# Half of the output projection's products of four token tiles computed inside Hyena's transform stage

## The chip, the cores and the metric

The kernel runs on one core of one Trainium2 chip. The metric is the device time of one execution in microseconds. Engines are called as in the profile: PE (TensorE, matmuls), DVE (VectorE), ACT (ScalarE), POOL (GpSimd) and SP (SyncE, which here issues the DMAs).

## The reference

One layer of a diffusion backbone over 1024 latent tokens of width 1024 and 256 context tokens. Four token mixers read one normalised input; their outputs, 256 columns each, are joined and go through one output projection. A routed mixture of 16 experts follows.

```python
ya_c, ya_l = gla_mixer(...)
yb_c, yb_l = hyena_mixer(...)
yc_c, yc_l = mamba_mixer(...)
yd_c, yd_l = deltanet_mixer(...)
y_l = jnp.concatenate([ya_l, yb_l, yc_l, yd_l], axis=-1) @ w_out[i]
x = x + (g1 * rmsnorm(y_l, norm_g[i, 1]).astype(F32)).astype(x.dtype)
h_l = modulate(x, norm_g[i, 2], sh2, sc2)
m_l = ec_moe(h_l, moe_router[i], moe_w_gate[i], moe_w_up[i], moe_w_down[i])
x = x + (g2 * rmsnorm(m_l, norm_g[i, 3]).astype(F32)).astype(x.dtype)
```

Hyena convolves its input twice with long filters, each time by a transform of length 2 x 1024, a product with the filter's spectrum and an inverse transform:

```python
def long_conv(u, h_fwd, h_bwd, d_skip):
    spec = jnp.fft.rfft(u, n=2 * l_, axis=1) * jnp.fft.rfft(kern, axis=0)[None]
    y = jnp.fft.irfft(spec, n=2 * l_, axis=1)[:, :l_]
    return y + u * d_skip
z = x1 * long_conv(v, h[:, 0, 0], h[:, 0, 1], d[0])
return (x2 * long_conv(z, h[:, 1, 0], h[:, 1, 1], d[1])).astype(u.dtype)
```

## The kernel before

The program is a row of stages. Every stage gives each engine its own list of instructions, which it runs in the order written; semaphores tie the lists together, and a stage begins when all engines have ended the one before. Nothing reorders work at run time, so the order around the change is what the code of a stage says.

Four stages matter. `hy_f` makes the filters' spectra by matmuls and, at its end, the transforms of Hyena's first two units. `hy_d` (called the transform stage below) does the rest of Hyena. `out` is the output projection with the router. Then `moe` runs the experts, one after the other.

**The transform stage.** Work is cut into eight units u = 4 o + 2 g + b: the convolution o, the half g of the 256 columns, the half b of the frequencies. For each unit PE makes the forward transform (`forward`, L2791, here called spectrum(u)), ACT copies one half of it out of PSUM (`hy_odd`, L3039), and DVE does sixteen operations, L3053 to L3079: two that add and subtract the halves (`hy_ab`, `hy_cd`, one operand in PSUM), and fourteen with both operands in SBUF, the product with the spectrum of the filter among them. Between groups of these DVE waits for its own last result, six times in a unit. Then PE makes the inverse transform inverse(u) (L3005, or L3010 in the second convolution), which adds into PSUM banks 4 and 5 for g = 0 and 6 and 7 for g = 1. When both b of a half are in, DVE multiplies them by the gate: `gated(g)` (L3083, into `hy_v`) after the first convolution, `result(g)` (L3091, into `yT`) after the second. DVE's order is unit 0, 1, 2, gated(0), 3, 4, gated(1), 5, 6, result(0), 7, result(1). PE's order is spectrum 2 and 3, inverse 0, 1 and 2, spectrum 4 and 5, inverse 3 and 4, spectrum 6 and 7, inverse 5, 6 and 7. POOL has nothing to do in this stage. SP loads the inverse's table and `w_out` in two halves of 2 MB, the first rows (k below 4) after spectrum(7), because their place is in use until then.

**The projection.** y = yT' w_out with 8 token tiles t of 128 and 8 blocks k of 128 input columns. Float32 is reached by three products of rounded halves: with hi the operand copied to the matmul's rounded type (ACT) and lo the rest (a subtraction on DVE or POOL), each block adds hi x hi, hi x lo and lo x hi, for two halves of 512 output columns. So a tile has 8 x 3 x 2 = 48 matmuls of 128x512 (L3221 to L3223). `w_out` is split at the start, eight blocks, by ACT (L3279) and DVE (L3316). `yT` is split tile by tile: `yT_hi` by ACT (L3284), `yT_lo` by POOL (L3176).

Behind the products of tile t comes a chain: squares and root of y on ACT (L3263, L3265), scaling on DVE (L3369, `res_tmp`), the residual sum on POOL (L3182, `x`), squares and root again on ACT (L3270, L3272), scaling on DVE (L3354, `h`), a row added on POOL (L3185, `h`) and a store for the experts. PE transposes x (`turn_rows`, L3196), ACT and DVE copy the transposes (`h2T`, L3300, L3341), and PE multiplies them by the router (L3209); softmax and a transpose of the affinities follow (L3293, L3336, L3217).

The lists fix who goes first. On PE, tile t is: half of its products, the router of tile t-2, the other half, turn_rows(t-1), the affinities' transpose of t-3. Before its first product PE waits for `yT_lo` of tile t. On POOL the order is yT_lo(t+1), x(t), h(t), yT_lo(t+2), x(t+1), and so on. On ACT it is yT_hi(t+1), the exponential of t-2, h2T(t-1), squares of y(t), squares of x(t). Two tiles use PSUM banks 0 to 3 in turn.

Of the kernel before, what the change touches and what calls it, by code (L numbers as in the profile page):

```python
# [15 lines left out]
F32 = mybir.dt.float32  # L16
# [2734 lines left out]
def hyena(nc, S, A, norm):  # L2751
# [43 lines left out]
    fwd_in, y_back = nc.alloc_semaphore("hy_fwd_in"), nc.alloc_semaphore("hy_y_back")  # L2795
    with Stage(nc, "hy_f", "tables turn_in d_in centre conv_1 conv_2 x2 taps tapped first skipped mixed even odd copied turned added_even "
# [13 lines left out]
        def _(sp):  # L2810
# [144 lines left out]
    S.w_out = Plan(nc, S.hT_at + KD * D * 4, S.stage_at).take("w_out", [P, KD, D])  # L2955
    plan = Plan(nc, high)
    with Stage(nc, "hy_d", "tab w_out fwd even odd_half ab x p yc pq w inv z fin") as s:
# [7 lines left out]
        X8 = X[:, :, :, :].rearrange("p s q c -> p (s q) c")  # L2965
        UNITS = [(u, u // (2 * BT), u // BT % 2, u % BT) for u in range(4 * BT)]

        def load_out(sp, h):
            sp.dma_start(S.w_out[:, 4 * h:4 * h + 4, :],
                         A["w_out"][0, 512 * h:512 * h + 512, :].rearrange("(k p) n -> p k n", p=P)).then_inc(s.w_out, 16)  # L2970

        @s.block.sync
        def _(sp):
            for q in range(2):
                sp.dma_start(inv[:, q, :, :], A["dft_inv"][q].rearrange("(t p) k -> p t k", p=P)).then_inc(s.tab, 16)
            load_out(sp, 1)
# [7 lines left out]
        def _(pe):  # L2984
# [30 lines left out]

            spectrum(2)
# [15 lines left out]
        @s.block.scalar
        def _(act):
            for u, o, g, b in UNITS:
# [72 lines left out]
    SPENT.extend([fwd_in, win_in, y_back] + S.hy_w)  # L3107
# [3 lines left out]
KEPT = (0, 1, 4, 5)  # L3111


def project_out(nc, S, A):
# [3 lines left out]
    xt = [low.take(f"res_x{b}", [P, D]) for b in range(2)]  # L3118
    tm = [low.take(f"res_tmp{b}", [P, D]) for b in range(2)]
    yh = [low.take("yT_hi0", [P, KD, P], F32R)]  # L3120
    yl = nc.alloc_sbuf_tensor_at("yT_lo", [P, KD, SEQ], F32R, offset=S.yT_at)
    wl = nc.alloc_sbuf_tensor_at("w_out_lo", [P, KD, D], F32R, offset=S.hT_at + KD * D * 4)
# [4 lines left out]
    wh = low.take("w_out_hi", [P, KD, D], F32R)  # L3127
# [9 lines left out]
    with Stage(nc, "out", "rows_in r_in x_in*2 y ss rt y_sc x1d ss2 rt2 h2m h2d h2s*2 tr ht_a ht_v lg mx ex af at at_o "  # L3137
                          "chain zero zst yh yl wh wl rr_in rr_t rc rs shift shifted x1h lgd h2l") as s:
# [751 lines left out]
```

## Time and profile before

| | us |
|---|---|
| median of 3 runs | 1743.55 |
| lowest and highest | 1738.53 and 1744.39 |
| the profiled execution | 1743.24 |
| its span, first to last instruction | 1741.4 |
| granted PE clock, mean over the span | 0.946 of full speed |
| busy: PE, DVE, ACT, POOL | 1540.7, 1207.1, 919.7, 307.9 |
| PE's share of the span | 88% |

The profile gives times from the start of the span. The transform stage lies from 871.5 to 957 us, the projection from 957 to 1087, the experts behind it. A line such as `1046.46 0.50 PE L3221 MATMUL ... [0.20 <-POOL yT_lo L3176]` reads: at 1046.46 us, for 0.50 us, PE ran line 3221 of the kernel, after 0.20 us of idling that POOL's write of yT_lo (line 3176) ended. Matmuls overlap, so their durations (0.39) are longer than the distance from one start to the next (0.227). In a merged row "x32" stands for 32 instructions, and the duration covers all of them.

### The profile page before, as it was taken

The numbers are of one execution on the slowest core, as the hardware profiler recorded it, in microseconds if no ns is written. First come the engines' busy times: TensorE is split into PE (matmuls) and PEld (weight loads), VectorE is DVE, ScalarE is ACT, GpSimd is POOL, SyncE is SP. The second block draws the span as 40 slices with busy tenths as digits, with TensorE's granted clock in tenths as the row PEclk, the third lists the DMA queues.
The fourth block names the chain that finished last, engine by engine and source line by source line (L and its number), as shares of the span: only waits on it lengthen the run. The fifth ranks groups of instructions, "written<-read, shape, count | busy, mean of one in ns | idle before, by whom it ended". The sixth has DMA issues, their size and how long they took to land. (4 is left out here: it accounts for less than half of the span.)

```text
span 1741.4 us, 21707 instructions
## 1 busy us (share of the span) xinstructions
PE 1540.7 (88%) x8298; PEld 1258.9 (72%) x8298; DVE 1207.1 (69%) x1403; ACT 919.7 (53%) x1308; POOL 307.9 (18%) x371
## 2 busy tenths in 40 slices
PE   6899999988989699998976999199999999999991
PEld 3686788777877589876475787078888888888871
DVE  4872754395655556665798534888888888888873
ACT  5441364375446376543100444167777777777753
POOL 0300500160016685000000443000100010001001
PEclk9999999998998899999988998599999999999996
DMA  9571210050018544211121522389999999999967
GB/s 351 165 263 55 114 49 1 25 168 27 1 41 256 185 113 122 89 32 61 61 97 49 208 96 74 153 341 394 392 376 402 395 389 381 401 396 395 377 216 217
DMA packets 109098, 345.13 MB, mean 198 GB/s; under 512 B 37501, under 2 KB 46998, under 8 KB 84419
## 3 DMA queue, kind: packets, MB, share of 16 engines
q1 hardware_dynamic: 99534, 320.34, 48.6%
q0 software_dynamic: 5328, 18.88, 4.5%
q10 hardware_dynamic: 4133, 4.53, 1.0%
q8 instruction: 66, 1.08, 0.3%
q14 instruction: 37, 0.30, 0.1%
HBM read 301.14 MB, written 37.32 MB: 194 GB/s over the span
## 5 line engine op out<-in xcount | busy, mean ns | idle before, releaser
L3635 DVE TENSOR_TENSOR w_lo<-w_raw,w_hi 128x2048 fp32r<-128x2048 f32 x192 | 438.1, 2291 | 64.1 <-ACT w_hi L3577 64.1
L3577 ACT ACTIVATE w_hi<-w_raw 128x2048 fp32r<-128x2048 f32 x192 | 368.1, 1918 | 142.9 <-PE ps L3522 132.7
L3520 PE MATMUL ps<-w_hi,xsT_hi 128*128 128x512 f32 x512 | 202.1, 395 | 1.1 <-DVE xsT_lo L3640 1.1
L3522 PE MATMUL ps<-w_hi,xsT_lo 128*128 128x512 f32 x512 | 199.8, 390 | 0.0
L3521 PE MATMUL ps<-w_lo,xsT_hi 128*128 128x512 f32 x512 | 199.5, 390 | 0.0
L3488 POOL DMA_INDIRECT moe_sum<-y,idx_col x15 | 30.3, 2021 | 461.0 <-ACT y L3597 430.0
L3520 PEld LDWEIGHTS ps<-w_hi,xsT_hi 128*128 128x128 f32 x512 | 96.2, 188 | 20.6 <-DVE xsT_lo L3640 1.5
L3522 PEld LDWEIGHTS ps<-w_hi,xsT_lo 128*128 128x128 f32 x512 | 96.1, 188 | 20.3
L3521 PEld LDWEIGHTS ps<-w_lo,xsT_hi 128*128 128x128 f32 x512 | 96.2, 188 | 19.3
L3520 PE MATMUL ps<-w_hi,hiddenT_hi 128*128 128x512 f32 x256 | 99.7, 390 | 0.6 <-DVE hiddenT_lo L3652 0.6
L3521 PE MATMUL ps<-w_lo,hiddenT_hi 128*128 128x512 f32 x256 | 99.6, 389 | 0.0
L3522 PE MATMUL ps<-w_hi,hiddenT_lo 128*128 128x512 f32 x256 | 99.6, 389 | 0.0
L3176 POOL TENSOR_TENSOR yT_lo<-yT,yT_hi 128x1024 fp32r<-128x1024 f32 x7 | 18.4, 2629 | 231.4 <-ACT yT_hi L3284 231.4
L3520 PEld LDWEIGHTS ps<-w_hi,hiddenT_hi 128*128 128x128 f32 x256 | 48.0, 188 | 11.0 <-DVE hiddenT_lo L3652 1.0
L3522 PEld LDWEIGHTS ps<-w_hi,hiddenT_lo 128*128 128x128 f32 x256 | 48.0, 188 | 10.0
L3521 PEld LDWEIGHTS ps<-w_lo,hiddenT_hi 128*128 128x128 f32 x256 | 48.0, 188 | 10.0
L3221 PE MATMUL ps<-w_out_hi,yT_hi 128*128 128x512 f32 x128 | 52.2, 408 | 2.1 <-POOL yT_lo L3176 2.1
L655 PE MATMUL ps<-hT_lo,mb_w_hi 128*128 128x512 f32 x128 | 50.5, 395 | 0.0
L3222 PE MATMUL ps<-w_out_lo,yT_hi 128*128 128x512 f32 x128 | 50.4, 394 | 0.0
L3223 PE MATMUL ps<-w_out_hi,yT_lo 128*128 128x512 f32 x128 | 50.3, 393 | 0.0
L1876 POOL TENSOR_TENSOR dn_block_inv<-dn_block_inv,dn_block_tmp 128x247 f32<-128x247 f32 (+15 forms) x82 | 46.8, 571 | 6.4
L757 ACT ACTIVATE mb_c_line<-ps 128x512 f32<-128x512 f32 (+1 forms) x20 | 18.3, 917 | 52.7 <-PE ps L660 49.9
(610 smaller groups left out, 3612.2 us busy)
## 6 DMA issues: line engine op xcount, KB each, us to landing
w_raw<-in_moe_w_gate SPq DMA_DIRECT2D x64, 1024.0 KB, 6.5
w_raw<-in_moe_w_up SPq DMA_DIRECT2D x64, 1024.0 KB, 8.2
w_raw<-in_moe_w_down SPq DMA_DIRECT2D x64, 1024.0 KB, 8.5
w_mod_row<-in_w_mod SPq DMA_DIRECT2D x32, 512.0 KB, 4.9
w_mod<-in_w_mod SPq DMA_DIRECT2D x8, 1024.0 KB, 17.6
dn_ma<-dn_ma SPq DMA_DIRECT2D x16, 512.0 KB, 4.0
dn_mT<-dn_ma SPq DMA_DIRECT2D x20, 256.0 KB, 3.6
x_tile<-in_x SPq DMA_DIRECT2D x8, 512.0 KB, 16.0
```

The lines of the kernel that those rows point to most:

```text
L655: nc.tensor.matmul(pairs(c), ring[:, i % 2, k, :], S.h_low[:, k, t0:t0 + 512].rearrange("p (a b) -> p a b", a=2), start=False, stop=False)
L1876: last = ops.tensor_tensor(bd[:, j + 1:DB, 0:c], bd[:, j + 1:DB, 0:c], t, ALU.subtract)
L3176: nc.gpsimd.tensor_tensor(tile_cols(yl, t + 1), tile_cols(S.yT, t + 1), yh[(t + 1) % 2][:, :, :], ALU.subtract).then_inc(s.yl, 1)
L3221: nc.tensor.matmul(out, yh[t % 2][:, k, :], wh[:, k, c], start=(k == 0), stop=False)
L3222: nc.tensor.matmul(out, yh[t % 2][:, k, :], wl[:, k, c], start=False, stop=False)
L3223: return nc.tensor.matmul(out, yl[:, k, t * P:(t + 1) * P], wh[:, k, c], start=False, stop=(k == KD - 1))
L3488: pool.indirect_dma_start(A["moe_sum"], bass.IndirectOffsetOnAxis(ap=S.icol[:, u:u + 1], axis=0), y[:, :], None, compute_op=ALU.add).then_ ...
L3520: nc.tensor.matmul(out, h[:, kk, :], wh[w][:, c:c + 512], start=kk == 0, stop=False)
L3521: nc.tensor.matmul(out, h[:, kk, :], wl[w][:, c:c + 512], start=False, stop=False)
L3522: last = nc.tensor.matmul(out, l[:, kk, :], wh[w][:, c:c + 512], start=False, stop=kk == KD - 1)
L3577: nc.scalar.activation(wh[q % RING][:, :], S.raw[q % RAW][:, :], ACT.Copy).then_inc(s.hi, 1)
L3635: nc.vector.tensor_tensor(wl[q % RING][:, :], S.raw[q % RAW][:, :], wh[q % RING][:, :].bitcast(F32), ALU.subtract).then_inc(s.lo, 1)
```

## The change

For the four odd token tiles (`PART`), the products of blocks 4 to 7, whose `yT` columns come from mixers that are done before (`y_kept`), are computed in the transform stage, and added in the projection.

- SP: the half of `w_out` with blocks 4 to 7 is loaded at the end of `hy_f`, when its last odd products are done.
- ACT in the transform stage: after `even` of unit 0 four copies that make `w_out_hi_rest`; after that of unit 1 four that make the odd tiles' `yT_hi_part` (128x512 each); later four copies `put(j)` of results (128x1024) out of PSUM banks 6 and 7 into `y_part`.
- POOL in the transform stage: four subtractions of 128x1024 (`w_out_lo`) and four of 128x512 (`yT_lo`), each waiting for ACT's copy.
- PE in the transform stage: `part(j)`, 24 matmuls of 128x512 each into banks 6 and 7: part(0) after inverse(1), part(1) after inverse(3), part(2) after inverse(5), part(3) after inverse(6).
- Banks 6 and 7 are now the parts', so both halves g use banks 4 and 5, and inverse(2), inverse(4) and inverse(6) first wait for gated(0), gated(1) and result(0).
- The projection: odd tiles have 24 matmuls and half-sized splits; DVE adds `y_part` to their PSUM banks before ACT squares them; `w_out` has four blocks to split; even tiles begin with blocks 4 to 7.

The diff, cut to its core:

```diff
@@ hyena, stage hy_f @@
+            sp.wait_ge(s.odd, BT)
+            load_out(sp, 1)
@@ stage hy_d, sync @@
-            load_out(sp, 1)
-
             sp.wait_ge(s.fwd, 4 * BT - 2)
             load_out(sp, 0)
@@ tensor @@
             def inverse(u):
                 u, o, g, b = UNITS[u]
                 pe.wait_ge(s.w, u + 1)
+                if b == 0 and (o, g) == (0, 1):
+                    pe.wait_ge(s.z, 1)
+                if b == 0 and (o, g) == (1, 0):
+                    pe.wait_ge(s.z, 2)
+                if b == 0 and (o, g) == (1, 1):
+                    pe.wait_ge(s.fin, 2)
                 for r in range(CLASSES):
-                    bank, at = 4 + 2 * g + r // 2, (r % 2) * 256
+                    bank, at = 4 + r // 2, (r % 2) * 256
...
+            def part(j):
+                pe.wait_ge(s.w_lo, 4)
+                pe.wait_ge(s.y_lo, j + 1)
+                if j:
+                    pe.wait_ge(s.put, j)
+                y_low = tile_of(yl, PART[j])
+                for k in range(4):
+                    for h in range(2):
+                        out, c = S.ps[:, 6 + h, :], slice(h * 512, h * 512 + 512)
+                        nc.tensor.matmul(out, yh[j][:, k, :], wh[:, k, c], start=(k == 0), stop=False)
+                        nc.tensor.matmul(out, yh[j][:, k, :], wl[:, 4 + k, c], start=False, stop=False)
+                        last = nc.tensor.matmul(out, y_low[:, k, :], wh[:, k, c], start=False, stop=(k == 3))
+                last.then_inc(s.part, 1)
@@ scalar @@
+                if u == 0:
+                    act.wait_ge(w_out_in, 16)
+                    for k in range(4):
+                        nc.scalar.activation(wh[:, k, :], wo[:, 4 + k, :], ACT.Copy).then_inc(s.w_hi, 1)
+                if u == 1:
+                    act.wait_ge(y_back, 16 * len(KEPT))
+                    for j, t in enumerate(PART):
+                        nc.scalar.activation(yh[j][:, :, :], tile_of(S.yT, t), ACT.Copy).then_inc(s.y_hi, 1)
+                if u in (3, 5):
+                    put(u // 2 - 1)
+            put(2)
+            put(3)
@@ gpsimd @@
+            for k in range(4):
+                pool.wait_ge(s.w_hi, k + 1)
+                nc.gpsimd.tensor_tensor(wl[:, 4 + k, :], wo[:, 4 + k, :], wh[:, k, :], ALU.subtract).then_inc(s.w_lo, 1)
+            for j, t in enumerate(PART):
+                pool.wait_ge(s.y_hi, j + 1)
+                nc.gpsimd.tensor_tensor(tile_of(yl, t), tile_of(S.yT, t), yh[j][:, :, :], ALU.subtract).then_inc(s.y_lo, 1)
@@ project_out @@
+        cut = lambda t: slice(0, 4 if t in PART else KD)
+        def order(t):
+            return (0, 1, 2, 3) if t in PART else (4, 5, 6, 7, 0, 1, 2, 3)
@@ vector @@
+                if t in PART:
+                    dve.wait_ge(s.y, t + 1)
+                    y = S.ps[:, 2 * (t % 2):2 * (t % 2) + 2, :].rearrange("p a b -> p (a b)")
+                    nc.vector.tensor_tensor(y, y, S.part[PART.index(t)][:, :], ALU.add).then_inc(s.joined, 1)
                 if t >= 1:
                     turn(t - 1)
```

How the instructions stand, at three places. PE in the transform stage, from the forward transforms at the end of `hy_f` on; the products with `yT_hi_part` are the first of part(0), eight such threes in all:

```order
 L2791 MATMUL ps<-hy_v,hy_fwd 128x128 x64
-L3005 MATMUL ps<-hy_w,hy_inv 128x128 x48
+L3024 MATMUL ps<-hy_w,hy_inv 128x128 x32
+L3044 MATMUL ps<-w_out_hi_rest,yT_hi_part_9303 128x512
+L3045 MATMUL ps<-w_out_lo,yT_hi_part_9303 128x512
+L3046 MATMUL ps<-w_out_hi_rest,yT_lo 128x512
```

Three inverses stood in a row; now a part stands between the second and the third, and in the same way behind inverse(3), inverse(5) and inverse(6).

POOL, from the last stage before Hyena's spectra into the projection, before:

```order
 L559 MEMSET hy_c_line_8443 128x1
-L3176 TENSOR_TENSOR yT_lo<-yT,yT_hi_9775 128x8x128
-L3182 TENSOR_TENSOR x_89<-res_tmp_9765,res_x_9763 128x1024
-L3185 TENSOR_TENSOR h_0_9770<-h_0_9770,row_broadcasts 128x1024
-L3176 TENSOR_TENSOR yT_lo<-yT,yT_hi_9767 128x8x128
```

and now:

```order
+L3099 TENSOR_TENSOR w_out_lo<-w_out,w_out_hi_rest 128x1024 x4
+L3102 TENSOR_TENSOR yT_lo<-yT,yT_hi_part_9303 128x4x128
+L3102 TENSOR_TENSOR yT_lo<-yT,yT_hi_part_9304 128x4x128
+L3102 TENSOR_TENSOR yT_lo<-yT,yT_hi_part_9305 128x4x128
+L3102 TENSOR_TENSOR yT_lo<-yT,yT_hi_part_9306 128x4x128
+L3242 TENSOR_TENSOR yT_lo<-yT,yT_hi_9929 128x4x128
+L3248 TENSOR_TENSOR x_89<-res_tmp_9927,res_x_9925 128x1024
+L3251 TENSOR_TENSOR h_0_9920<-h_0_9920,row_broadcasts 128x1024
+L3242 TENSOR_TENSOR yT_lo<-yT,yT_hi_9919 128x8x128
```

Eight subtractions of the transform stage stand ahead of the projection's; in the projection the subtraction for an odd tile is half as large (4 blocks), that for an even tile is the same.

## Rows read from the trace of the kernel before

**Rows 1.** Windows, the two stages: PE, PEld, DVE, ACT, POOL busy; clock, DMA.

```profile
871.50:957.00 85.50, 60.52 (x384) 56.15 (x384) 78.53 (x135) 4.78 (x8) 0.00 (x0) 0.86 0.20 74
957.00:1087.00 130.00, 122.39 (x617) 101.82 (x617) 58.79 (x100) 63.37 (x103) 51.60 (x21) 0.95 0.35 126
```

**Rows 2.** Timeline of DVE, transform stage: start, us, line, [idle before <-releaser].

```profile
872.28 0.69 DVE L3053 TENSOR_TENSOR hy_ab<-ps,hy_odd 128x512 f32<-128x512 f32 x1 [0.78 <-ACT hy_odd L3039]
...
881.47 0.68 DVE L3053 TENSOR_TENSOR hy_ab<-ps,hy_odd 128x512 f32<-128x512 f32 x1
...
899.81 1.21 DVE L3083 TENSOR_TENSOR hy_v<-hy_x,ps 128x1024 f32<-128x1024 f32 x1
...
938.77 2.07 DVE L3091 TENSOR_TENSOR yT<-yT,ps 128x512 f32<-128x512 f32 x2
...
953.88 1.10 DVE L3091 TENSOR_TENSOR yT<-yT,ps 128x512 f32<-128x512 f32 x1 [3.87 <-PE ps L3010]
```

**Rows 3.** Timeline of PE, transform stage.

```profile
873.72 6.43 PE L2791 MATMUL ps<-hy_v,hy_fwd 128*128 128x128 f32 x32 [5.36 <-DVE hy_cd L3054]
...
899.95 5.33 PE L3005 MATMUL ps<-hy_w,hy_inv 128*128 128x128 f32 x32 [4.64 <-DVE hy_w L3079]
...
912.26 3.74 PE L3005 MATMUL ps<-hy_w,hy_inv 128*128 128x128 f32 x32
...
938.91 3.72 PE L3010 MATMUL ps<-hy_inv,hy_w 128*128 128x256 f32 x16 [3.47 <-DVE hy_w L3079]
950.06 5.80 PE L3010 MATMUL ps<-hy_inv,hy_w 128*128 128x256 f32 x16 [7.43 <-DVE hy_w L3079]
```

**Rows 4.** Timeline of PE in the projection, around the starts of tiles.

```profile
1002.06 1.03 PE L3196 MATMUL ps<-tables,x 128*128 128x128 f32 x8
...
1017.80 0.50 PE L3221 MATMUL ps<-w_out_hi,yT_hi 128*128 128x512 f32 x1 [0.74 <-POOL yT_lo L3176]
...
1028.66 0.39 PE L3221 MATMUL ps<-w_out_hi,yT_hi 128*128 128x512 f32 x1
...
1030.70 1.03 PE L3196 MATMUL ps<-tables,x 128*128 128x128 f32 x8
...
1046.46 0.50 PE L3221 MATMUL ps<-w_out_hi,yT_hi 128*128 128x512 f32 x1 [0.20 <-POOL yT_lo L3176]
```

**Rows 5.** Timeline of ACT and POOL, the chain behind tile 2.

```profile
1005.61 0.29 ACT L3265 ACTIVATE out_stats<-out_stats,eps 128x1 f32<-128x1 f32 x1
...
1007.49 2.37 POOL L3182 TENSOR_TENSOR x<-res_tmp,res_x 128x1024 f32<-128x1024 f32 x1 [6.08 <-DVE res_tmp L3369]
...
1013.04 2.39 POOL L3185 TENSOR_TENSOR h<-h,row_broadcasts 128x1024 f32<-128x1024 f32 x1 [3.17 <-DVE h L3354]
...
1015.38 2.36 POOL L3176 TENSOR_TENSOR yT_lo<-yT,yT_hi 128x1024 fp32r<-128x1024 f32 x1
```

**Rows 6.** Timelines of ACT and DVE around the squares of tile 7.

```profile
1073.74 1.02 ACT L3263 ACTIVATE squares<-ps 128x1024 f32<-128x1024 f32 x1 [1.05 <-PE ps L3223]
...
1071.40 1.37 DVE L3336 TENSOR_SCALAR aff<-aff,out_stats 128x16 f32<-128x16 f32 x1
```

**Rows 7.** Windows, ahead of inverse(7); columns as in rows 1.

```profile
948.00:950.00 2.00, 0.00 (x0) 0.00 (x0) 1.97 (x5) 0.00 (x0) 0.00 (x0) 0.50 0.00 0
```

**Rows 8.** Where POOL's and DVE's operations meet: timelines, one row of a source view.

```profile
959.55 9.16 DVE L3316 TENSOR_TENSOR w_out_lo<-w_out,w_out_hi 128x1024 fp32r<-128x1024 f32 x8
...
966.79 4.17 POOL L3176 TENSOR_TENSOR yT_lo<-yT,yT_hi 128x1024 fp32r<-128x1024 f32 x1 [231.38 <-ACT yT_hi L3284]
...
L3322 DVE TENSOR_TENSOR router_scaled<-router,row_cols x2: 277/1278/2278, 968.8 to 971.0; 128x128 f32<-128x128 f32 x2
...
75.14 3.95 POOL L989 TENSOR_TENSOR hT_lo<-hT,hT_hi_end 128x512 fp32r<-128x512 f32 x2
...
75.85 8.49 DVE L1213 SCALAR_TENSOR_TENSOR mod_acc<-w_mod_row,silu_cond,mod_acc 128x1024 f32<-128x1024 f32 x5
```

**Rows 9.** DMA view, 800 to 975 us: KB each, median us from issue to landing.

```profile
w_out<-in_w_out SPq DMA_DIRECT2D x2, 2048.0 KB, 9.8
```

More of the change, by code:

```diff
@@ L2954, in hyena @@
     assert low.at <= S.hT_at + KD * D * 4
-    S.w_out = Plan(nc, S.hT_at + KD * D * 4, S.stage_at).take("w_out", [P, KD, D])
+    S.w_out_low = nc.alloc_sbuf_tensor_at("w_out_lo", [P, KD, D], F32R, offset=S.hT_at + KD * D * 4)
+    S.y_low = nc.alloc_sbuf_tensor_at("yT_lo", [P, KD, SEQ], F32R, offset=S.yT_at)
+    S.w_out_rest = nc.alloc_sbuf_tensor_at("w_out_hi_rest", [P, 4, D], F32R, offset=low.at)
+    assert low.at + 4 * D * 4 == S.hT_at + KD * D * 4
+    wo, wl, wh, yl = S.w_out, S.w_out_low, S.w_out_rest, S.y_low
+    yh = [nc.alloc_sbuf_tensor_at(f"yT_hi_part{j}", [P, 4, P], F32R, offset=S.stage_at - (4 - j) * 2048)
+          for j in range(len(PART))]
+    S.part = [nc.alloc_sbuf_tensor_at(f"y_part{j}", [P, D], F32, offset=at)
+              for j, at in enumerate((SBUF_END - 8288, SBUF_END - 4192, S.spare_at, S.spare_at + 4096))]
     plan = Plan(nc, high)
-    with Stage(nc, "hy_d", "tab w_out fwd even odd_half ab x p yc pq w inv z fin") as s:
+    with Stage(nc, "hy_d", "tab fwd even odd_half ab x p yc pq w inv z fin w_hi w_lo y_hi y_lo part put") as s:
         W = plan.take("hy_w", [P, 2, BT, CLASSES, 2, P])
@@ L3020, in _ @@
             inverse(1)
+            part(0)
             inverse(2)
@@ L3024, in _ @@
             inverse(3)
+            part(1)
             inverse(4)
@@ L3028, in _ @@
             inverse(5)
+            part(2)
             inverse(6)
+            part(3)
             inverse(7)
@@ L3033, in _, with put @@
         def _(act):
+            def put(j):
+                act.wait_ge(s.part, j + 1)
+                nc.scalar.activation(S.part[j][:, :], S.ps[:, 6:8, :].rearrange("p a b -> p (a b)"), ACT.Copy).then_inc(s.put, 1)
             for u, o, g, b in UNITS:
@@ L3117, in project_out @@
     rows = low.take("row_broadcasts", [P, 3, D])
-    xt = [low.take(f"res_x{b}", [P, D]) for b in range(2)]
-    tm = [low.take(f"res_tmp{b}", [P, D]) for b in range(2)]
     yh = [low.take("yT_hi0", [P, KD, P], F32R)]
-    yl = nc.alloc_sbuf_tensor_at("yT_lo", [P, KD, SEQ], F32R, offset=S.yT_at)
-    wl = nc.alloc_sbuf_tensor_at("w_out_lo", [P, KD, D], F32R, offset=S.hT_at + KD * D * 4)
+    yl, wl = S.y_low, S.w_out_low
     low = Plan(nc, S.hT_at + 2 * KD * D * 4)
@@ L3126, in project_out @@
     st = low.take("out_stats", [P, LT, 8])
-    wh = low.take("w_out_hi", [P, KD, D], F32R)
+    w_first = low.take("w_out_hi_first", [P, 4, D], F32R)
+    wh = [w_first[:, k, :] for k in range(4)] + [S.w_out_rest[:, k, :] for k in range(4)]
+    xt = [low.take(f"res_x{b}", [P, D]) for b in range(2)]
+    tm = [low.take(f"res_tmp{b}", [P, D]) for b in range(2)]
     yh.append(low.take("yT_hi1", [P, KD, P], F32R))
@@ L3230, in _ @@
             pe.wait_ge(s.yl, 1)
-            for k in range(KD):
-                pe.wait_ge(s.wl, k + 1)
+            for k in order(0):
+                if k < 4:
+                    pe.wait_ge(s.wl, k + 1)
                 for h in range(2):
@@ L3248, in _ @@
                     if t < LT:
-                        for k in range(KD):
+                        for k in order(t):
                             last = product(t, h, k)
@@ L3277, in _ @@
             nc.scalar.activation(yh[0][:, :, :], tile_cols(S.yT, 0), ACT.Copy).then_inc(s.yh, 1)
-            for k in range(KD):
-                nc.scalar.activation(wh[:, k, :], wo[:, k, :], ACT.Copy).then_inc(s.wh, 1)
+            for k in range(4):
+                nc.scalar.activation(wh[k], wo[:, k, :], ACT.Copy).then_inc(s.wh, 1)
             for t in range(LT + 2):
@@ L3313, in _ @@
             nc.vector.tensor_tensor(tile_cols(yl, 0), tile_cols(S.yT, 0), yh[0][:, :, :], ALU.subtract).then_inc(s.yl, 1)
[L3314 removed]
+            for k in range(4):
                 dve.wait_ge(s.wh, k + 1)
[L3316 removed]
+                nc.vector.tensor_tensor(wl[:, k, :], wo[:, k, :], wh[k], ALU.subtract).then_inc(s.wl, 1)
             dve.wait_ge(s.rr_t, 1)
```

43 lines of the change are left out of this document (27 added, 16 removed).

## The prediction

> **What bounds the kernel now.** I read the stretches first: the Hyena transform stage (871.5 to 957 us) and the output projection (957 to 1087 us) [rows 1]. In the transform stage DVE is busy for 78.5 of 85.5 us and PE for 60.5. The rows of DVE there show why: a unit (16 operations) takes 9.19 us (872.28 to 881.47), one follows the other without a gap, and DVE has its only long wait (3.87 us) at the end, for PE's inverse(7) [rows 2]. So DVE sets this stage, PE has gaps of 3.4 to 7.4 us [rows 3], and work that goes into the gaps is free only if it keeps DVE free as well.
>
> In the output projection PE is busy for 122.4 of 130 us [rows 1], which looks like the bound. The rows around the tiles' starts say something finer [rows 4]. y(t) is the moment at which a tile's products end, read off the transposes that follow. Tile 2 ends at 1002.06 and tile 4 starts at 1017.80, released by POOL's yT_lo; tile 4 ends at 1030.70 and tile 6 starts at 1046.46, released by the same; 15.74 and 15.76 us. Between lies a chain over four engines [rows 5]: turn_rows (1.0) and ACT's h2T, squares and root to 1005.90, DVE's res_tmp, POOL's x to 1009.86, ACT's squares and root again, DVE's h, POOL's h to 1015.43, and only then POOL's yT_lo of tile t+2 to 1017.74. An even tile's own products and router take 12.9 us (1017.80 to 1030.70). So start(t+2) = start(t) + 12.9 + 15.7 = 28.6 us for two tiles; the rows give 1046.46 - 1017.80 = 28.66. PE is full there because the odd tile between happens to fill the 15.7 us: the loop through POOL is already the bound, and PE is level with it.
>
> **The change part by part.**
>
> *Products out of the projection.* Four tiles lose 24 of 48 products. At 0.227 us from one to the next (1028.66 to 1030.70 for nine) that is 5.45 us a tile, 21.8 us of PE's time. The tiles are the odd ones. An even tile still has 48 products, and its chain still ends with a whole yT_lo, so even tiles still start 28.6 us apart. The odd tile's 5.45 us becomes a longer wait of PE. I book 0 of the 21.8 us for tiles 1, 3 and 5.
>
> *Tile 7.* Here nothing of an even tile follows, so 5.45 us could show. But ACT comes to the squares of y(7) at 1073.74 only 0.2 us after PE, behind squares of x(6), an exponential and two table loads; DVE reaches its new addition only after the affinity of tile 5, which ends at 1072.77 [rows 6]. The addition of 128x1024 costs about 1.2 us (DVE's hy_v, with one PSUM operand, takes 1.21 [rows 2]), so it ends near 1074.0 and the squares begin 0.3 us later than before. Gain 0, loss 0.3 to 0.5; up to 2 if the router's and the transposes' small products there run at the lower clock. I take 0.5.
>
> *PE's new wait inside the projection.* After tile t (even) PE now does turn_rows, half a tile with a router and another turn_rows: 1.3 + 5.45 + 1.7 + 1.0 = 9.4 us, and then waits for the rest of the 15.7 us: 6.3 us, before tiles 4 and 6, and about as long before tile 2, whose products wait for the same subtraction behind tile 0's chain. What such a wait costs can be read in the transform stage: after 7.43 us of idling inverse(7) took 5.80 us where inverse(6), the same sixteen, took 3.72 [rows 3], and the granted clock had fallen to 0.50 by 948 to 950 [rows 7]. That is the level of 1.2 GHz in place of 2.4. Against 3.74 for 32 products at full clock, the wait of 5.36 us cost 2.7 and that of 4.64 cost 1.6; the wait of 3.47 cost nothing [rows 3]. I take 2.1 for each of three restarts, 6.3 us, on the path, since the even tile's products are a link of the loop. Bounds 0 and 3 x 2.7 = 8.1.
>
> *ACT in the transform stage.* Four copies of 128x1024 after `even` of unit 0, four half as large after that of unit 1, and four copies of results; ACT's pass over 128x1024 takes 1.02 us [rows 6], so some 10 us in all. ACT is otherwise busy for 4.8 of 85.5 us [rows 1]; the copy for unit 1 is needed at 881.47 and now comes near 872.2 + 4 x 1.02 = 876.3. Free. The load of w_out that they wait for is now issued in the stage before, when its last odd products have ended; such a load takes 9.8 us [rows 9]. Were it 3 us late, the copy for unit 1 would still be in time. Free.
>
> *POOL in the transform stage.* Eight subtractions with two SBUF operands, four of 128x1024 (2.37 us each when alone) and four of half that. They run beside DVE, which is the bound, and 14 of the 16 operations of a unit read two SBUF operands. The trace shows what this does [rows 8]. POOL's subtraction issued at 966.79 took 4.17 us, waited until DVE's w_out_lo series had ended (968.71) and then ran to 970.96; DVE's router_scaled, issued at 968.82, took 2.278 us where its twin took 0.277: 2.0 us lost. At 75.14 two POOL subtractions of 128x512 went in between five chained DVE operations: 8.49 us for five of some 1.2 each (as hy_v's 1.21), so 2.4 lost, about 1.2 for each. Both engines stand still for one another, a whole instruction at a time, and POOL gets its turn where DVE waits for its own last result. A unit has six such places, so POOL's eight go through in units 0 and 1. The first starts behind ACT's first copy, near 873.3, and costs 2.0; three more at about 2.25 (968.71 to 970.96) cost 6.75; of the small ones one falls on a pair that reads PSUM (hy_ab, hy_cd) and three cost 1.2. Sum 12.3; the small ones' share is the least sure, and I use 12. Bounds: 0, if DVE were not held, and 4 x 2.37 + 4 x 1.2 = 14.3. Nothing hides it: from unit 2 on everything shifts.
>
> The Trainium skill, "SBUF — State Buffer", section "Who interferes with whom", says that the second port pair is an exclusive lock, that a VectorE operation with two SBUF inputs and a GpSimd operation contend for it, and that the loser waits for the whole instruction. By that rule alone the eight would cost their whole length, 14.3 in place of 12 (1763 in place of 1761); the rows agree with it in kind, and the difference is the part that runs beside operations with a PSUM operand.
>
> *Two banks for both halves.* inverse(2), inverse(4) and inverse(6) now wait for DVE's reading of the banks. Before, inverse(2) began at 899.95 and inverse(6) at 938.91, and DVE's readings ended at 901.02 and 940.84 [rows 2, 3]. They move by 1.1 and 1.9 us (with the parts ahead of them not much more), and PE then has to finish spectrum(4) and spectrum(6) before units 4 and 6. Counted through with products of 0.227 us and full clock: spectrum(6) ends 0.9 us before unit 6 wants it. Cost 0. Behind inverse(6), part(3) ends some 0.6 us after unit 7: +0.6.
>
> *A warm end.* part(3) runs right up to inverse(7), which then takes 3.7 instead of 5.8 us and is on the path [rows 2, 3]: -2.1.
>
> **Sum.** Transform stage +12.0 + 0.6 - 2.1 = +10.5; projection +6.3 + 0.5 = +6.8; together +17.3 us. The profiled execution took 1743.24 us with a span of 1741.4, the median is 1743.55. Behind the projection come DVE's selection and the experts, which only start later. 1743.55 + 17.3 = 1760.9; I say 1761, 1.0% slower.
>
> **The rivals.**
> 1. *No holding of DVE* (POOL's subtractions slip in without cost): transform stage -1.5, projection +6.8, 1749. For it: w_out_lo's eight ran on at 1.15 us each (9.16 in all) with POOL already waiting [rows 8]. Against: those were a series without waits, a unit is not. 0.10.
> 2. *No fall of the clock in the projection's waits*: 1743.55 + 10.5 + 0.5 = 1754.5. For it: the one wait of 3.47 us that cost nothing; against: all three waits of over 4 us cost 1.6 or more. 0.12.
> 3. *POOL starves*: it gets its turn only beside hy_ab and hy_cd, once per unit. Then yT_lo's first part is ready only after unit 3, part(0) holds back inverse(2) and spectrum(4) in PE's queue, and unit 4, due at 910, would start after 1.2 (the subtraction) + 7.5 (part(0), half of it at the lower clock) + 3.7 + 3.7 us of work from 914 on, near 930: +20 and 3.6 of holding beside the pairs, less the 2.1 at the end, with 6.8 in the projection: near 1771. 0.08.
> 4. *PE is the bound of the projection, so it is faster*: the 21.8 us come off, with 10.5 us of the transform stage against them: 1732. It decides from the point where the chain to yT_lo takes less than an odd tile's stay on PE (9.4 us after the change, and it takes 15.7). For it: 122 of 130 us busy, and waits for yT_lo of only 0.74 and 0.20 us [rows 1, 4]. Against: the two equal intervals of 28.6 us. 0.06.
>
> **How the numbers follow.** Forecast 0.64, rivals 0.10, 0.12, 0.08 and 0.06. The range runs from rival 1 to the forecast with the upper bounds (14.3 for 12, 8.1 for 6.3, 2 for 0.5: 1767): 1748 to 1767, with the forecast, rival 2 and most of rival 1, 0.83. A measurement of this kernel can tell about 0.3% (5.2 us) from no change. Faster by more: 0.05; within: 0.08 (rival 1 ends on this edge); slower: 0.87.
>
> **What would show it.** In the profile after: DVE's units 0 and 1 together 30 us instead of 18, with single operations of 2.5 us or more beside POOL's; units 2 to 7 at 9.2 us as before; PE's last inverse at 3.7 us; even tiles starting 30 to 31 us apart and waiting about 6 us for yT_lo, with a granted clock near 0.5 behind each wait; DVE's new addition before ACT's squares of tile 7. I am wrong if even tiles start much less than 28 us apart, or if units 0 and 1 keep their 9.2 us.

## The result and the profile after

The changed kernel took 1762.98 us in the median of 4 runs (1760.93 to 1764.0), the kernel before 1743.9 us in 4. The ratio is 1.0109, with a 95% interval of 1.0094 to 1.0125: slower by 19.1 us. The prediction was 1761 us, slower, in a range of 1748 to 1767.

The profiled execution of the changed kernel took 1762.85 us with a span of 1761.0, 19.6 more than before. I cut both spans at the same three marks: the start of ACT's first `hy_odd` (start of the transform stage), its first `yT_hi` of the projection, and DVE's first MAX8 of the selection that follows. For the kernel before these windows are (columns as in [rows 1]: start and end, length, busy PE, PEld, DVE, ACT, POOL, granted clock, DMA):

```profile
871.58:957.05 85.47, 60.52 (x384) 56.15 (x384) 78.53 (x134) 4.78 (x8) 0.00 (x0) 0.86 0.20 74
957.05:1088.55 131.50, 122.39 (x617) 101.82 (x617) 58.79 (x101) 63.37 (x103) 51.60 (x21) 0.94 0.35 125
```

and for the changed kernel:

```profile
872.35:968.18 95.83, 76.90 (x480) 70.00 (x480) 90.97 (x134) 14.62 (x20) 17.32 (x8) 0.88 0.12 44
968.18:1107.80 139.62, 109.20 (x521) 90.37 (x521) 54.77 (x101) 57.96 (x99) 45.37 (x21) 0.85 0.33 118
```

| part | before | after | difference |
|---|---|---|---|
| up to the transform stage | 871.58 | 872.35 | +0.8 |
| transform stage | 85.47 | 95.83 | +10.4 |
| projection | 131.50 | 139.62 | +8.1 |
| from the selection to the end of the span | 652.9 | 653.2 | +0.3 |

The 0.8 us ahead of the transform stage tell nothing. In the ten profiles of this case that stage begins between 870.9 and 875.9 us; the four kernels that load `w_out` where the kernel before does span that whole range, the six that load half of it earlier lie inside it.

So the projection has lost 13 us of PE's busy time (122.39 to 109.20, with 96 products fewer) and has become 8.1 us longer. In the transform stage DVE does the same 134 operations in 90.97 us instead of 78.53, and POOL, idle before, is busy for 17.32.

**Transform stage.** DVE's unit 0 in the changed kernel; the first row is one of the pair with an operand in PSUM, the other (L3116) is left out. In the kernel before such a unit took 9.19 us [rows 2]:

```profile
873.04 0.69 DVE L3115 TENSOR_TENSOR hy_ab<-ps,hy_odd 128x512 f32<-128x512 f32 x1 [0.78 <-ACT hy_odd L3080]
...
874.37 2.32 DVE L3120 TENSOR_TENSOR hy_x<-hy_ab 128x256 f32<-128x256 f32 x1
876.61 2.59 DVE L3121 TENSOR_TENSOR hy_x<-hy_ab 128x256 f32<-128x256 f32 x1
879.12 2.56 DVE L3122 TENSOR_TENSOR hy_x<-hy_cd 128x256 f32<-128x256 f32 x1
881.61 2.56 DVE L3123 TENSOR_TENSOR hy_x<-hy_cd 128x256 f32<-128x256 f32 x1
884.20 2.17 DVE L3126 TENSOR_TENSOR hy_p<-hy_x,hy_k_cos 128x1024 f32<-128x1024 f32 x1
886.29 2.28 DVE L3126 TENSOR_TENSOR hy_p<-hy_x,hy_k_sin 128x1024 f32<-128x1024 f32 x1
888.60 1.63 DVE L3131 TENSOR_TENSOR hy_p<-hy_p,hy_p 128x512 f32<-128x512 f32 x1
890.16 1.74 DVE L3132 TENSOR_TENSOR hy_p<-hy_p,hy_p 128x512 f32<-128x512 f32 x1
...
894.61 0.68 DVE L3115 TENSOR_TENSOR hy_ab<-ps,hy_odd 128x512 f32<-128x512 f32 x1
```

and all of POOL's work in that stage:

```profile
874.04 9.85 POOL L3099 TENSOR_TENSOR w_out_lo<-w_out,w_out_hi_rest 128x1024 fp32r<-128x1024 f32 x4 [138.27 <-ACT w_out_hi_rest L3085]
883.85 7.51 POOL L3102 TENSOR_TENSOR yT_lo<-yT,yT_hi_part 128x512 fp32r<-128x512 f32 x4
```

Eight of DVE's operations, one after the other, are long, and POOL has eight subtractions. The unit takes 894.61 - 873.04 = 21.57 us, 12.38 more than 9.19. From 894.61 on units take 9.2 us again. At the end of the stage PE's last inverse, inverse(7), runs at full clock:

```profile
963.26 3.72 PE L3029 MATMUL ps<-hy_inv,hy_w 128*128 128x256 f32 x16
```

It took 5.80 us before [rows 3] and now takes 3.72. That gives back 2 us: 12.38 - 2.0 = 10.4.

**Projection.** The starts and ends of tiles on PE; an end is read off the transposes (`tables,x`) that follow, as in [rows 4]:

```profile
1000.19 0.79 PE L3291 MATMUL ps<-w_out_hi_rest,yT_hi 128*128 128x512 f32 x1 [6.57 <-POOL yT_lo L3242]
1000.78 0.63 PE L3292 MATMUL ps<-w_out_lo,yT_hi 128*128 128x512 f32 x1
1001.21 0.63 PE L3293 MATMUL ps<-w_out_hi_rest,yT_lo 128*128 128x512 f32 x1
...
1005.88 0.40 PE L3292 MATMUL ps<-w_out_lo,yT_hi 128*128 128x512 f32 x1
1006.12 0.40 PE L3293 MATMUL ps<-w_out_hi_first,yT_lo 128*128 128x512 f32 x1
...
1015.68 1.03 PE L3262 MATMUL ps<-tables,x 128*128 128x128 f32 x8
...
1031.39 0.79 PE L3291 MATMUL ps<-w_out_hi_rest,yT_hi 128*128 128x512 f32 x1 [6.15 <-POOL yT_lo L3242]
...
1046.66 1.03 PE L3262 MATMUL ps<-tables,x 128*128 128x128 f32 x8
...
1062.36 0.79 PE L3291 MATMUL ps<-w_out_hi_rest,yT_hi 128*128 128x512 f32 x1 [4.12 <-POOL yT_lo L3242]
...
1077.50 1.03 PE L3262 MATMUL ps<-tables,x 128*128 128x128 f32 x8
```

Even tiles start 31.20 and 30.97 us apart, where [rows 4] have 28.66. From the end of tile 2 to the start of tile 4 it is 15.71 us and from tile 4 to tile 6 15.70, as before (15.74, 15.76): the chain over ACT, DVE and POOL has kept its length. What has grown is the tile itself, 12.90 before, now 15.49, 15.27 and 15.14. Behind the first product, twelve start 0.43 us apart (as 1000.78 and 1001.21), the later ones about 0.23 (1005.88 to 1006.12). The granted clock in the windows says the same (columns as above):

```profile
996.00:998.00 2.00, 0.00 (x0) 0.00 (x0) 1.08 (x2) 1.41 (x3) 2.00 (x2) 1.00 0.00 0
1002.00:1004.00 2.00, 2.00 (x6) 1.54 (x5) 0.00 (x0) 1.47 (x4) 0.46 (x1) 0.50 0.52 199
```

PE is idle from 993.6 on. At 996 to 998 the clock still stood at 2.4 GHz (1.00); behind the wait it stands at 1.2 GHz (0.50). PE's waits for `yT_lo` in one view (in total, how often, the longest):

```profile
PE ps L3291 <- POOL yT_lo L3242: 16.8, 3, 6.6
```

They came to 2.1 us in three waits before. Another wait is new: behind tile 7 PE has no work until the router, and finds itself at the lower clock there:

```profile
1094.11 3.57 PE L3275 MATMUL ps<-router_scaled,h2T 128*128 128x16 f32 x16 [5.04 <-ACT h2T L3375]
```

Before, the row at this place was:

```profile
1075.81 2.32 PE L3209 MATMUL ps<-router_scaled,h2T 128*128 128x16 f32 x16 [0.90 <-ACT h2T L3300]
```

### The profile page after: what moved, and what is told of

The parts are those of the page before. It is cut to its first block and busy times, and to the rows that moved or that the text cites. A ratio compares the mean times of both kernels' runs of the same rounds, so it can differ in the third digit from the quotient of the medians.

```text
span 1761.0 us, 21736 instructions
## 1 busy us (share of the span) xinstructions
PE 1545.7 (88%) x8298; PEld 1262.9 (72%) x8298; DVE 1217.1 (69%) x1403; ACT 924.6 (53%) x1316; POOL 319.5 (18%) x379
## 5 line engine op out<-in xcount | busy, mean ns | idle before, releaser
L2791 PE MATMUL ps<-hy_v,hy_fwd 128*128 128x128 f32 x256 | 33.9, 300 | 20.6 <-DVE hy_cd L3116 20.6
L2791 PEld LDWEIGHTS ps<-hy_v,hy_fwd 128*128 128x128 f32 x256 | 33.5, 215 | 21.5 <-DVE hy_cd L3116 15.4
L1874 POOL TENSOR_TENSOR dn_block_tmp<-dn_block_l,dn_block_inv 128x247 f32<-128x247 f32 (+15 forms) x82 | 44.0, 537 | 6.4
L233 PE MATMUL ps<-tables 128*128 128x256 f32 x134 | 39.0, 454 | 4.8 <-PEq L209 1.8
## 6 DMA issues: line engine op xcount, KB each, us to landing
x_tile<-in_x SPq DMA_DIRECT2D x8, 512.0 KB, 15.7
```

Source lines behind the costliest of these rows:

```text
L233: nc.tensor.matmul(S.ps[:, bank, 0:256], S.t("ident"), S.tab[:, 0:256], start=True, stop=True)
L1874: ch(ops.tensor_tensor(t, bl[:, j + 1:DB, j:j + 1].to_broadcast([P, i, c]), bd[:, j:j + 1, 0:c].to_broadcast([P, i, c]), ALU.mult))
L2791: last = nc.tensor.matmul(S.ps[:, 2 * (u % 2) + r // 2, at:at + P], fwd[:, q, nt, b * P:(b + 1) * P], v[:, nt, g * P:(g + 1) * P], start=( ...
```

## Experiments

My theory is the prediction's: two costs that add up, POOL's subtractions holding DVE in the transform stage, and in the projection a loop through POOL's `yT_lo` that makes the removed products worthless and puts PE's restarts at the lower clock on the path. Rivals are a slow transform stage for another reason (PE's added products, the shared banks), and a projection that is slow for another reason than the loop. Ratios are against the kernel before, run on the same chip beside them: for the first four below 11 runs with a median of 1743.81 us, for the other four 27 runs with a median of 1745.12.

### Half the products left out, nothing else

The kernel before; the odd tiles' products of blocks 4 to 7 are not computed at all, so y lacks half of them.

```diff
-                        for k in range(KD):
+                        for k in range(4 if t % 2 else KD):
                             last = product(t, h, k)
```

(In these tiles the mark that ends the sum in PSUM moves to the last block that is left.)

> The kernel before, with the products of blocks 4 to 7 of the four odd token tiles left out of the projection and computed nowhere (24 of 48 matmuls of those tiles; their y lacks these blocks). Nothing is added to the transform stage. My theory (the loop through POOL's yT_lo bounds the projection): even tiles still wait for POOL and start 31 us apart, 28.6 plus a restart at the lower clock of 2.4; the whole takes 7 to 9 us longer than before, near 1752. Rival (PE bounds the projection): even tiles start about 23 us apart and the whole takes 1722, 21.8 less.

1751.89 us (5 runs), ratio 1.0054 (1.0032 to 1.0075). A kernel that does 21.8 us less of PE's work, and nothing in exchange, is slower by 8 us. Its tiles 2 and 4:

```profile
988.53 0.79 PE L3221 MATMUL ps<-w_out_hi,yT_hi 128*128 128x512 f32 x1 [6.56 <-POOL yT_lo L3176]
...
1004.29 1.03 PE L3196 MATMUL ps<-tables,x 128*128 128x128 f32 x8
...
1019.99 0.79 PE L3221 MATMUL ps<-w_out_hi,yT_hi 128*128 128x512 f32 x1 [6.14 <-POOL yT_lo L3176]
```

Its waits are those of the changed kernel (6.57 and 6.15), the even tiles start 31.46 us apart, and tile 2 takes 15.76 us. This removes the rival in which PE bounds the projection, and every explanation of the projection by what the transform stage does.

### POOL writes instead of subtracting

The changed kernel; POOL's eight subtractions are memsets of the same tiles, so the low parts are zero.

```diff
-                nc.gpsimd.tensor_tensor(wl[:, 4 + k, :], wo[:, 4 + k, :], wh[:, k, :], ALU.subtract).then_inc(s.w_lo, 1)
+                nc.gpsimd.memset(wl[:, 4 + k, :].bitcast(F32), 0.0).then_inc(s.w_lo, 1)
```

(and the same for `yT_lo`.)

> The changed kernel, with POOL's eight subtractions in the transform stage replaced by memsets of the same tiles (the low parts of these blocks are zero, all waits stay): POOL writes SBUF and reads nothing there. Theory A (DVE is held only by POOL instructions that read SBUF too): unit 0 falls from 21.6 to 9.2 us, the whole to 1750.5. Theory B (any POOL instruction on SBUF holds DVE for its length, here about 0.95 and 0.5 us): unit 0 takes some 15 us and the whole 1756. Theory C (the hold has nothing to do with POOL, unit 0 is slowed by ACT's copies or PE's waits): unit 0 stays at 21.6, 1763.

1749.02 us (7 runs), ratio 1.0027 (1.0012 to 1.0041). POOL works at the same place, on the same outputs, and DVE doesn't notice:

```profile
875.05 3.72 POOL L3099 MEMSET w_out_lo<- 128x1024 f32 x4 [138.66 <-ACT w_out_hi_rest L3085]
878.82 2.08 POOL L3102 MEMSET yT_lo<- 128x512 f32 x4
```

```profile
874.08 0.69 DVE L3115 TENSOR_TENSOR hy_ab<-ps,hy_odd 128x512 f32<-128x512 f32 x1 [0.78 <-ACT hy_odd L3080]
...
875.75 0.42 DVE L3121 TENSOR_TENSOR hy_x<-hy_ab 128x256 f32<-128x256 f32 x1
...
883.27 0.68 DVE L3115 TENSOR_TENSOR hy_ab<-ps,hy_odd 128x512 f32<-128x512 f32 x1
```

Unit 0 takes 9.19 us, L3121 0.42 us instead of 2.59. The stage is shorter than before the change:

```profile
873.38:956.81 83.43, 76.85 (x480) 69.91 (x480) 78.56 (x134) 14.62 (x21) 5.80 (x8) 0.94 0.14 51
```

83.43 against 85.47 us: ACT's copies, PE's 96 added products, the gates for the shared banks and the earlier load cost nothing, and the warm last inverse gives 2.0 back. So DVE is held by POOL's subtractions, which read two operands in SBUF, and not by POOL's being busy or by its writes. This run does not part the reading from the arithmetic. The same section of the Trainium skill that the prediction draws on ("SBUF — State Buffer", "Who interferes with whom") has it so: a VectorE operation with two SBUF inputs contends with a GpSimd instruction that reads SBUF, not with one that only writes. By the medians the difference to the changed kernel is 1762.98 - 1749.02 = 14 us, in the profiles of the stage 12.4.

### The same subtractions on DVE

The changed kernel; the eight subtractions stand in DVE's list between unit 0 and unit 1, and POOL has none.

```diff
             unit(0)
+            low_parts()
             unit(1)
             unit(2)
```

> The changed kernel, with the eight subtractions of the transform stage on DVE between units 0 and 1, none on POOL. If the 12.4 us come from two engines excluding each other, they are replaced by DVE's own time, 4 x 1.15 + 4 x 0.62 = 7.1 us: whole 1757.7, 5.3 less than the changed kernel. If POOL's subtractions cost DVE nothing and the loss has another source, this is 7 slower than it, 1770.

1757.73 us (2 runs), ratio 1.0078 (1.0048 to 1.0107), as expected. On DVE they take 6.95 us (881.30 to 888.25, where the next unit begins):

```profile
881.30 4.63 DVE L3150 TENSOR_TENSOR w_out_lo<-w_out,w_out_hi_rest 128x1024 fp32r<-128x1024 f32 x4
885.85 2.49 DVE L3153 TENSOR_TENSOR yT_lo<-yT,yT_hi_part 128x512 fp32r<-128x512 f32 x4
```

Handing them to POOL, the idle engine, cost DVE 12.4 us; doing them itself costs DVE 7.0.

### PE kept busy ahead of the even tiles

The changed kernel; before it waits for tiles 2, 4 and 6, PE does nine products of 128x256 whose result nothing reads.

```diff
+                if t in (2, 4, 6):
+                    pe.wait_ge(s.y_sc, t - 1)
+                    for _ in range(9):
+                        nc.tensor.matmul(S.ps[:, 0, 256:512], S.t("ident"), S.tab[:, 0:256], start=True, stop=True)
                 if t < LT:
                     pe.wait_ge(s.yl, t + 1)
```

> The changed kernel, with nine extra products of 128x256 by a table (about 4.1 us at full clock, into a free PSUM bank) on PE ahead of the wait of tiles 2, 4 and 6. If the even tiles take 15.1 to 15.5 us in place of 12.9 because PE's clock has fallen in the wait, they take 12.9 again and the whole 1756, 7 less. If they are longer for another reason (the other order of the blocks, the place of the operands), they stay at 15.3 and the whole at 1763.

1759.36 us (2 runs), ratio 1.0087 (1.0058 to 1.0116). By its median 3.6 us less than the changed kernel, where about 7 was expected; two runs leave that loose. In the profile the projection takes 133.90 us, 5.7 less:

```profile
1001.72 0.50 PE L3291 MATMUL ps<-w_out_hi_rest,yT_hi 128*128 128x512 f32 x1 [2.68 <-POOL yT_lo L3242]
...
1014.59 1.03 PE L3262 MATMUL ps<-tables,x 128*128 128x128 f32 x8
...
1030.31 0.50 PE L3291 MATMUL ps<-w_out_hi_rest,yT_hi 128*128 128x512 f32 x1 [2.07 <-POOL yT_lo L3242]
...
1044.77 1.03 PE L3262 MATMUL ps<-tables,x 128*128 128x128 f32 x8
```

Tile 2 takes 12.87 us, its length at full clock, and the chain behind it is still 15.7 us (1014.59 to 1030.31). Tile 6 found `yT_lo` ready behind the filler and took 12.86 us (1060.48 to 1073.34). So the growth of the tiles is the clock. Tile 4, however, took 14.46 us though its wait was the shorter one: the filler did not cure it, and the clock says where it fell, 0.8 us after PE had begun again:

```profile
1030.00:1031.00 1.00, 0.69 (x3) 0.61 (x4) 0.00 (x0) 0.98 (x3) 0.26 (x1) 1.00 1.03 389
1031.00:1032.00 1.00, 1.00 (x5) 0.74 (x4) 0.09 (x1) 0.86 (x2) 0.00 (x0) 0.53 0.99 258
```

That is why 5.7 us came back and not 7.2. Why this wait of 2.07 us was followed by a fall and that of 2.68 us wasn't stays open.

### The loop cut: yT_lo two tiles ahead, in the changed kernel

On ACT, `yT_hi` of tile t+2 moves up between the squares of y(t) and of x(t); on POOL, `yT_lo` of tile t+2 moves up between x(t) and h(t). No work is added or removed.

```diff
                 if t < LT - 1:
                     square_y(act, t)
+                    if t + 2 < LT:
+                        high_part(t + 2)
                     square_x(act, t)
...
-                if t + 1 < LT:
-                    pool.wait_ge(s.yl, t + 1)
-                    pool.wait_ge(s.yh, t + 2)
...
+                if t + 2 < LT:
+                    low_part(t + 2)
                 pool.wait_ge(s.rows_in, 48)
```

> The changed kernel, with the split of tile t+2 moved forward in the projection: ACT makes yT_hi(t+2) between the squares of y(t) and those of x(t), where it waited, and POOL makes yT_lo(t+2) between x(t) and h(t), where it waited 3.2 us, instead of behind h(t). My theory (the loop through yT_lo is the bound, 15.7 us from y(t) to the start of t+2): yT_lo is ready 10.3 us after y(t), PE's own stay between two even tiles is about 10 us, so even tiles start about 23.2 us apart instead of 31, PE's clock stays up, and the whole takes 1740, 23 less than the changed kernel. Rival (the order of ACT's and DVE's lists ties the tiles as strongly as POOL did): even tiles stay 28 us or more apart and the whole above 1755.

1744.27 us (10 runs), ratio 0.9997 (0.9985 to 1.0009): some 19 us less than the changed kernel, level with the kernel before. The transform stage is as slow as in the changed kernel, the projection 20.1 us shorter:

```profile
874.69:970.50 95.81, 76.83 (x480) 69.93 (x480) 90.92 (x134) 14.62 (x21) 17.32 (x8) 0.88 0.12 44
970.50:1090.06 119.56, 102.07 (x521) 84.98 (x521) 59.58 (x100) 57.74 (x99) 45.72 (x21) 0.91 0.38 137
```

The wait for `yT_lo` is 1.07 us ahead of tile 2, 0.66 ahead of tile 4 and none ahead of tile 6. Some 3 of the 23 us expected did not come; PE now waits for the affinities from DVE (6.3 us in four waits); the longest stands right ahead of tile 6, which starts at 1046.69, 26.6 us behind tile 4, where tile 4 starts 23.1 behind tile 2:

```profile
1020.09 0.50 PE L3296 MATMUL ps<-w_out_hi_rest,yT_hi 128*128 128x512 f32 x1 [0.66 <-POOL yT_lo L3240]
...
1046.38 0.38 PE L3288 MATMUL ps<-tables,aff 128*32 128x128 f32 x2 [2.52 <-DVE affT L3430]
```

### The same cut in the kernel before

The same move with whole tiles.

> The kernel before, with the same move of yT_hi(t+2) and yT_lo(t+2). Here PE needs 14.2 us for a tile, 28.4 for two, and the loop took 28.6: only PE's waits for yT_lo (2.1 us in all) can go, so 1742, no difference that can be told. If it gains more than 5 us, PE was not level with the loop in the kernel before.

1742.57 us (10 runs), ratio 0.9991 (0.998 to 1.0002): no difference that can be told. The projection took 129.55 us, 2.0 less than before, with PE busy for 121.69 of them. With all products PE fills the loop; cutting the loop frees almost nothing. It is only with half of the odd tiles' products gone that the loop costs 20 us. Between the two cut kernels the removed products are worth 129.55 - 119.56 = 10.0 us of the 21.8, and PE waits 5 us more for the affinities in the changed one (6.3 against 1.3) and 3 us more for `h2T` (5.0 against 2.0).

### Both cures together

The changed kernel with the loop cut and the subtractions on DVE.

> The changed kernel, with the early split of tile t+2 and the eight subtractions of the transform stage on DVE between units 0 and 1. The two gains should add, since they lie in different stages: 23 and 5.3 less than the changed kernel, 1734.5. If the gain in the projection needs POOL's or DVE's time from elsewhere, less.

1738.04 us (6 runs), ratio 0.9958 (0.9945 to 0.997): faster than both kernels, by 0.4% and 1.5%. It is 3.5 us above what was expected; the gain in the projection fell short here as it did above. Its projection takes 119.74 us, its transform stage:

```profile
874.99:965.37 90.38, 76.63 (x480) 69.71 (x480) 85.51 (x142) 14.61 (x20) 0.00 (x0) 0.91 0.13 47
```

The first cure is worth 5.4 us in the transform stage with the loop cut (95.81 to 90.38) as without it (95.83 to 90.37), the second 20 us in the projection in either case: the two costs are separate and add up.

### The shared banks alone

The kernel before with both halves of the inverse in banks 4 and 5 and the waits that this needs; no product moved.

```diff
-                    bank, at = 4 + 2 * g + r // 2, (r % 2) * 256
+                    bank, at = 4 + r // 2, (r % 2) * 256
```

> The kernel before, with both halves of the inverse in banks 4 and 5 and the three new waits of inverse(2), inverse(4) and inverse(6), and nothing else of the change. I expect no cost: these inverses begin 1.1, 1.1 and 1.9 us later and spectrum(4) and spectrum(6) still end 0.2 us before DVE asks for them; transform stage 85.5 us, whole 1743.9. If the waits matter, DVE has gaps ahead of units 4 and 6 and the stage is 1 to 4 us longer.

1745.53 us (8 runs), ratio 1.0003 (0.9993 to 1.0013): no difference. In its trace inverse(2) starts 29.6 us after the stage's start instead of 28.4, near the 1.1 us worked out (first row), and inverse(6) starts 70.4 us after it instead of 67.3, 3.1 us later where 1.9 was worked out. It takes 6.30 us in place of 3.72, since it begins at the lower clock behind a wait of 6.02 us (second row; the third is inverse(7)):

```profile
902.41 6.24 PE L3011 MATMUL ps<-hy_w,hy_inv 128*128 128x128 f32 x32 [5.99 <-DVE hy_v L3089]
...
943.18 6.30 PE L3016 MATMUL ps<-hy_inv,hy_w 128*128 128x256 f32 x16 [6.02 <-DVE yT L3097]
952.26 5.20 PE L3016 MATMUL ps<-hy_inv,hy_w 128*128 128x256 f32 x16 [2.79 <-DVE hy_w L3085]
```

The stage grows from 85.47 to 85.83 us, and that is a sum of two terms. The gates did hold DVE: it idles ahead of unit 4, whose forward transform stands behind inverse(2) in PE's list and begins 2.1 us later than before (908.49), and its list is 1.0 us late from there to the end of unit 7:

```profile
912.32 0.69 DVE L3059 TENSOR_TENSOR hy_ab<-ps,hy_odd 128x512 f32<-128x512 f32 x1 [0.86 <-issue]
```

The last inverse, 5.20 us where it took 5.80, gives 0.6 back. The expectation's "no cost" is right for the whole and wrong for DVE. With the parts in PE's list the 1.0 us doesn't arise: in the run with memsets DVE's unit 7 begins as long after the stage's start as before, to 0.1 us.

## Why the prediction was right, point by point

**The two bounds.** Both readings held: DVE's list sets the transform stage, and the loop through POOL's `yT_lo` sets the projection. "I book 0 of the 21.8 us" is what half_left_out shows, and the 15.7 us from the end of an even tile to the next one's start stood unchanged in every kernel that kept the loop.

**POOL's holding of DVE** (booked 12, bounds 0 and 14.3): 12.38 us. The sum held, the place didn't. The prediction gave POOL its turns "where DVE waits for its own last result", so it spread the eight over units 0 and 1 and let one small subtraction fall beside the PSUM pair for nothing. In the trace POOL got a turn at each of eight successive boundaries between DVE's operations, right after the pair, and all eight went through in unit 0. Worked out from the rows: the four operations of 128x256 have grown from 0.42 us by 1.9 to 2.2 each, 8.3 together (booked 8.75); the next four from 1.22 and 0.69 us by about 1.0 each, 4.0 together (booked 1.2 for three, 3.6). Two small misses of opposite sign. The rule of the Trainium skill ("SBUF — State Buffer", section "Who interferes with whom") that the loser waits for the whole instruction is borne out in kind by these rows; full lengths would have made 14.3, and the rows show 12.4. The prediction gave another reason for its smaller sum, a part that would run beside operations with an operand in PSUM; only the first did so, for 0.3 us (874.04 to 874.33). All eight held up operations with two operands in SBUF, and each of the large ones cost DVE 0.2 to 0.5 us less than its own 2.37; what the rest of the difference is stays open. That booking and measurement are so close is in part luck.

**Part(3) behind unit 7** (booked +0.6): 0. Inverse(7) followed unit 7 at once, at 963.26 behind 963.21. **The warm end** (booked -2.1): -2.0. Together the stage came to +10.4, booked +10.5.

**The restarts** (booked 3 x 2.1, bounds 0 and 8.1): 2.6, 2.4 and 2.2, together 7.2 from the lengths of the tiles. The price was the one read behind the wait of 7.43 us, between 1.6 and 2.7 behind two others; waits of 6.6 and 6.2 us turned out nearer the dear end. The prediction read the kernel before too narrowly here: beside the wait of 3.47 us that cost nothing its trace has waits of 2.65 and 3.43 us that cost 1.6 and 1.7 (rows at the end). That bears on its rival 2, which leaned on the one free wait, and not on the sum. The last even tile waited only 4.12 us, since PE spent 1.42 us waiting for an affinity just ahead, and it still cost 2.2. Seen at the end of tile 6, relative to the stage's start, the projection is 7.0 us later.

**Tile 7** (booked 0.5, up to 2): 1.1 at the MAX8. The working named both parts and sized one of them. DVE's addition (1.22 us) came before the squares as foreseen and made them 0.2 us late, but the larger part is the router behind it, 3.57 us instead of 2.32 (1.25 more), because PE had idled for 5.04 us ahead of it. That was the case "if the router's small products run at the lower clock", and it should have been the booked one: the same working that takes 5.45 us of products from PE leaves it idle just there.

**Two banks, ACT, the load of w_out** (booked 0 each): 0 in the changed kernel, by the memsets, whose stage has all of them and is 2.0 us shorter than before. Alone, without the parts, the shared banks cost DVE 1.0 us and the stage 0.4.

**The sum.** +17.3 was booked; +19.1 measured, +19.6 in the profiles. Of the 2.3 us between booking and profile, 0.8 arose ahead of the transform stage and 0.35 behind the start of the selection, neither by a mechanism of the prediction; 0.7 is the restarts as they show at the end of tile 6 (7.0 for 6.3), 0.6 is tile 7, and the transform stage takes 0.15 off. Of the rivals, the one without holding (1749) is what the kernel with memsets gave (1749.02), and the one that is faster (1732) is out: even with the loop cut the changed kernel took 1744.27. The rival in which the clock does not fall is out by the window at 1002 to 1004, and POOL did not starve.

## What to carry to other kernels

Before moving work out of a stage, find the loop that sets it: an engine that is busy for 93% of a stage can be level with a chain over other engines, and taking its work away then buys nothing and may cost its clock. Work given to an idle engine is not free when it needs what the bound engine needs: here POOL's subtractions cost DVE 12.4 us, and the same subtractions on DVE itself 7.0. A change that only moves the bound elsewhere deserves a look at that other chain: here moving the split of `yT` up in two lists turned a loss of 1.1% into no difference, and with the other eight subtractions on DVE into a gain of 0.4%.

## What the runs showed of the hardware

- POOL's subtraction of two SBUF operands and DVE's operations on SBUF take turns at each boundary, also inside a group that DVE runs through without a wait: eight of eight in one unit, 2.1 us of DVE's time for 128x1024 and 1.0 for 128x512. In [rows 8] POOL had to wait through a series of DVE's subtractions; that did not happen here. What makes the difference is open. POOL's memsets of the same tiles (0.93 us for 128x1024, 0.52 for 128x512) held nothing up.
- The length of PE's last wait doesn't tell alone whether the clock falls. Products after waits of 3.47 us [rows 3] and 2.68 us (pe_kept_busy, tile 2) ran at 2.4 GHz; after waits of 2.07 us (pe_kept_busy, tile 4) and 2.79 us (two_banks_alone, the last inverse, 5.20 us instead of 3.7) they ran in part at 1.2 GHz. The kernel before has it twice as well, in spectrum(3), 5.37 us where 3.74 is the time of 32 such products at full clock [rows 3], and in inverse(4), 5.41 us where inverse(6) took 3.72:

```profile
882.80 5.37 PE L2791 MATMUL ps<-hy_v,hy_fwd 128*128 128x128 f32 x32 [2.65 <-DVE hy_cd L3054]
...
919.43 5.41 PE L3010 MATMUL ps<-hy_inv,hy_w 128*128 128x256 f32 x16 [3.43 <-DVE hy_w L3079]
```

- The clock can fall when PE is already at work again: 0.8 us behind the restart in pe_kept_busy (tile 4), and in the kernel before at inverse(4), which began at 919.43 with a granted clock of 1.00 from 919 to 920, 0.58 from 920 to 921 and 0.50 from 921 to 923. Which of two waits of like length is followed by a fall stays open.
